# The first two weight units after two of the norms are multiplied together, chunk by chunk, into four PSUM banks

## What is computed

```python
# first block: gated short convolution, then a squared-relu MLP
a = modulate(rmsnorm(h, g_pre), shift, scale)
h = h + gate * rmsnorm(short_gated_conv(a, w_in, conv, w_out), g_post)
f = squared_relu_mlp(modulate(rmsnorm(h, g_pre_ff), s2, c2), mlp_w_in, mlp_w_out)   # 1024 -> 4096 -> 1024
h = h + gate2 * rmsnorm(f, g_post_ff)
# second block, layer 0: forgetting attention and pooling, then a convolutional feed-forward
z = rms_norm(h, even_norm) @ even_w_in          # q, k, v, forget logit, pool input
h = h + concat(attention(q, k, v, cumsum(log_sigmoid(f + b))), pool(u)) @ even_w_out
h = h + conv_ffn(rms_norm(h, ffn_norm0))
# layer 1: conformer convolution, then a feed-forward
```

## Time and profile before

| what | value |
|---|---|
| runs, median (lowest to highest) | 1940.53 us (1940.49 to 1945.62), 3 runs |
| profiled execution, span | 1940.5 us |
| time around the span in that execution | none that the profile shows |
| PE busy | 1759.1 us, 91% |
| DVE busy | 1133.7 us, 58% |
| ACT busy | 705.6 us, 36% |
| chain that ended last | PE 86%, DVE 6%, ACT 3% |

### The profile page before, as it was taken

The page is one execution under the profiler, slowest core; times in us unless marked ns, Lnnn a source line. Parts: engine busy times, 40 slices in busy tenths (PEclk is TensorE's granted clock), DMA queues, the critical chain, the costliest instruction groups (busy, mean ns, idle before and its releaser), DMA issues.

```text
span 1940.5 us, 22187 instructions
## 1 busy us (share of the span) xinstructions
PE 1759.1 (91%) x7628; PEld 1411.7 (73%) x7628; DVE 1133.7 (58%) x1740; ACT 705.6 (36%) x1003; POOL 21.1 (1%) x52
## 2 busy tenths in 40 slices
PE   5899949999999499679899999989996989999997
PEld 4788838888888278567688888867652768888886
DVE  5698655343344653444664573757997567466364
ACT  2222235232222434542552442434323455234232
POOL 0000000000000000300000000000000000000000
PEclk7799879999999699899899999999997989999999
DMA  6576302332324022001223223232210222323221
GB/s 227 172 225 227 112 22 87 91 104 87 108 87 125 22 87 88 22 0 52 68 97 109 87 86 108 76 97 66 65 43 22 65 65 86 108 87 107 89 92 60
DMA packets 172276, 176.01 MB, mean 91 GB/s; under 512 B 2984, under 2 KB 171180, under 8 KB 172220
## 3 DMA queue, kind: packets, MB, share of 16 engines
q1 hardware_dynamic: 172220, 175.29, 28.2%
HBM read 173.15 MB, written 2.10 MB: 90 GB/s over the span
## 4 chain that ended last, share of the span: by engine, by line
PE 86%; DVE 6%; ACT 3%; issue 2%; DMA 1%; DVEq 0%; SPq 0%; ACTq 0%
PE PSUM L1128 25%; PE PSUM L1129 25%; PE PSUM L1130 25%; PE PSUM L1301 3%; DVE SQ L698 1%; PE PSUM L1254 1%; PE PSUM L1156 1%; PE PSUM L1148 1%; PE PSUM L1271 1%; DMA XROW<-in_x 1%; DVE X L747 1%; PE PSUM L1195 1%; DMA ARAW<-in_ada_w 1%; ACT L413 1%; PE PSUM L1255 0%
## 5 line engine op out<-in xcount | busy, mean ns | idle before, releaser
L1128 PE MATMUL PSUM<-XH,WH 128*128 128x512 f32 x1504 | 594.1, 395 | 30.9 <-DVE XL L729 15.2
L1129 PE MATMUL PSUM<-XL,WH 128*128 128x512 f32 x1504 | 589.4, 392 | 0.0
L1130 PE MATMUL PSUM<-XH,WL 128*128 128x512 f32 x1504 | 589.2, 392 | 0.0
L390 ACT ACTIVATE WH<-RAW 128x1024 fp32r<-128x1024 f32 x280 | 287.3, 1052 | 826.9 <-PE PSUM L1130 810.8
L1128 PEld LDWEIGHTS PSUM<-XH,WH 128*128 128x128 f32 x1504 | 285.4, 190 | 98.5 <-issue 39.4
L685 DVE TENSOR_TENSOR WL<-RAW,WH 128x1024 fp32r<-128x1024 f32 x280 | 335.4, 1222 | 17.7 <-ACT WH L390 17.7
L1129 PEld LDWEIGHTS PSUM<-XL,WH 128*128 128x128 f32 x1504 | 285.4, 190 | 61.0 <-issue 1.9
L1130 PEld LDWEIGHTS PSUM<-XH,WL 128*128 128x128 f32 x1504 | 284.9, 189 | 59.9
L1128 PE MATMUL PSUM<-HH,WH 128*128 128x512 f32 x672 | 264.6, 394 | 6.2 <-DVE HL L1007 5.8
L1129 PE MATMUL PSUM<-HL,WH 128*128 128x512 f32 x672 | 264.0, 393 | 0.0
L1130 PE MATMUL PSUM<-HH,WL 128*128 128x512 f32 x672 | 263.6, 392 | 0.0
(11 more groups left out here) (181 smaller groups left out, 1389.6 us busy)
## 6 DMA issues: line engine op xcount, KB each, us to landing
RAW<-in_ffn_w_up SPq DMA_DIRECT2D x44, 1024.0 KB, 5.1
ARAW<-in_ada_w SPq DMA_DIRECT2D x24, 1024.0 KB, 5.2
RAW<-in_mlp_w_in SPq DMA_DIRECT2D x16, 1024.0 KB, 5.7
RAW<-in_mlp_w_out SPq DMA_DIRECT2D x16, 1024.0 KB, 5.2
RAW<-in_ffn_w_down SPq DMA_DIRECT2D x16, 1024.0 KB, 5.1
RAW<-in_sc_w_in SPq DMA_DIRECT2D x12, 1024.0 KB, 5.2
RAW<-in_odd_w_pw SPq DMA_DIRECT2D x12, 1024.0 KB, 5.3
RAW<-in_even_w_in SPq DMA_DIRECT2D x8, 1024.0 KB, 5.8
```

What stands on the lines that cost most here:

```text
L390: act.activation(WH[:, j, a:b, :], RAW[:, j, a:b, :], ACT.Copy).then_inc(s_hi, 1)
L1128: pe.matmul(o, wh, mh[:, k, :], start=(k == 0), stop=False)
L1129: pe.matmul(o, wh, ml[:, k, :], start=False, stop=False)
L1130: mm = pe.matmul(o, wl, mh[:, k, :], start=False, stop=(k == kn - 1))
```

## The change

The preparation of the second unit of each of the two stages (units 17 and 49) moves ahead of the split: on ACT before `split_shift` and `split`, on DVE behind the first two scalings and ahead of the first `XL`. On PE a new function `two_units` takes units 16 and 17 (48 and 49) together: it waits until all banks are empty and both units' weights are complete, goes through chunks 0 to 4 with both units (12 matmuls per chunk, four banks), then through chunks 5 to 7 with the first unit, counts up `s_mm`, and through 5 to 7 with the second. The units 18, 19, 50 and 51 follow with `product` one by one, written out where they were in a hardware loop.

```diff
--- before.py
+++ after.py
@@ -465,8 +465,8 @@
             for c in range(DC):
                 square(ST_X1, c, X[:, c, :])
             rms(ST_X1, 1.0 / D)
+            prep_late(U_MLP + 1)
             split_shift(1, S_GS1, S_MOD + 24)
-            prep_late(U_MLP + 1)
 
 
             for g in range(4):
@@ -501,8 +501,8 @@
             rms(ST_X2, 1.0 / D)
             act.wait_ge(s_fw, 16)
             act.activation(FH[:, :, :], FRAW[:, :, :], ACT.Copy).then_inc(s_fh, 1)
+            prep_late(U_EVEN + 1)
             split(2, "even_norm", 0)
-            prep_late(U_EVEN + 1)
 
 
             act.wait_ge(e_f, 1)
@@ -712,7 +712,7 @@
                     dve.wait_ge(s_as, 7 * (summed(a)[0] - 1) + k)
                     stt(dst, w, s, dst, ALU.mult, ALU.add).then_inc(s_as if k < 7 else s_ad, 1)
 
-            def split(m, gs=None, gain=None, k=0):
+            def split(m, gs=None, gain=None, k=0, late=None):
 
                 dve.wait_ge(s_r, (ST_X0, ST_X1, ST_X2, ST_F0, ST_X3, ST_F1)[m] + 1)
 
@@ -721,6 +721,8 @@
 
                 scaled(0)
                 scaled(1)
+                if late is not None:
+                    prep_late(late)
                 for c in range(DC):
                     dve.wait_ge(sp_h, 8 * m + c + 1)
                     if gain is None:
@@ -854,8 +856,7 @@
                     tt(sc_(S_MG1, 8), sc_(S_MOD + 40, 8), col("gains", 24, 8), ALU.mult).then_inc(s_sm, 1)
                     dve.wait_ge(s_sm, 7)
             post_norm(ST_Y0, 0, S_MG0)
-            split(1)
-            prep_late(U_MLP + 1)
+            split(1, late=U_MLP + 1)
 
 
             for g in range(4):
@@ -884,8 +885,7 @@
             post_norm(ST_Y1, 1, S_MG1)
             dve.wait_ge(s_fh, 1)
             tt(FL[:, :, :], FRAW[:, :, :], FH[:, :, :].bitcast(F32), ALU.subtract).then_inc(s_fl, 1)
-            split(2, gain="even_norm")
-            prep_late(U_EVEN + 1)
+            split(2, gain="even_norm", late=U_EVEN + 1)
 
 
             dve.wait_ge(s_vin2, 16)
@@ -1130,6 +1130,24 @@
                         mm = pe.matmul(o, wl, mh[:, k, :], start=False, stop=(k == kn - 1))
                 mm.then_inc(s_mm, 1)
 
+            def two_units(u, base_):
+
+                pe.wait_ge(s_ev, u)
+                for j in range(2):
+                    pe.wait_ge(s_lo, (u + j) * 2 + 2)
+                for first, last, units in ((0, 5, (0, 1)), (5, 8, (0,)), (5, 8, (1,))):
+                    for k in range(first, last):
+                        pe.wait_ge(s_x, base_ + k + 1)
+                        for j in units:
+                            for c in range(2):
+                                wh, wl = (w[:, j, k, c * P:c * P + P] for w in (WH, WL))
+                                o = PS_[:, 2 * j + c, :]
+                                pe.matmul(o, wh, XH[:, k, :], start=(k == 0), stop=False)
+                                pe.matmul(o, wh, XL[:, k, :], start=False, stop=False)
+                                mm = pe.matmul(o, wl, XH[:, k, :], start=False, stop=(k == 7))
+                    if last == 8:
+                        mm.then_inc(s_mm, 1)
+
             def x_units(u0, n, base_):
 
                 with pe.Fori(0, n // 2) as it:
@@ -1199,7 +1217,12 @@
             channel_sum(ST_Y0)
             channel_sum(ST_X1)
             for g in range(4):
-                x_units(U_MLP + 8 * g, 4, 8)
+                if g == 0:
+                    two_units(U_MLP, 8)
+                    for j in range(2):
+                        product(U_MLP + 2 + j, j, XH, XL, 8, s_x, 8)
+                else:
+                    x_units(U_MLP + 8 * g, 4, 8)
                 h_units(U_MLP + 8 * g + 4, 4, 8 + 8 * g)
             channel_sum(ST_Y1)
             channel_sum(ST_X2)
@@ -1213,7 +1236,9 @@
                 pe.matmul(o, FH[:, k, :], XL[:, k, :], start=False, stop=False)
                 mm = pe.matmul(o, FL[:, k, :], XH[:, k, :], start=False, stop=(k == 7))
             mm.then_inc(s_f, 1)
-            x_units(U_EVEN, 4, 16)
+            two_units(U_EVEN, 16)
+            for j in range(2):
+                product(U_EVEN + 2 + j, j, XH, XL, 8, s_x, 16)
             def head_sums(n0):
 
                 for n in (n0, n0 + 1):
```

## The result

The changed kernel takes 1945.66 us (median of 20 runs, 1944.02 to 1947.27). The kernel before, run beside it, takes 1943.01 us (20 runs, 1939.43 to 1945.62). The ratio is 1.0014, 95% interval 1.0008 to 1.0021: 2.7 us slower, between 1.6 and 4.1 us. It is within the 0.3% that was called no change, and it is slower, as forecast.

A forecast was written before the change was run, and what follows sets the result against it. PE, at 91% of the span, was taken as the bound, with its waits ahead of first matmuls. Delays of 1.5 and 2.2 us less 0.2 us of clock gave +3.5 us on 1940.5 us: 1944.0 us, range 1942.0 to 1946.0 us.

The forecast's parts named there:

- The reordering is worth nothing: Reordering the 96 matmuls of the two units on PE gains and costs 0, in both stages.
- +1.5 us in stage 1: Before the MLP: preparation moved ahead of the split delays the first XL by 1.5 us.
- +2.2 us in stage 2: Before the even layer's projections: DVE's moved subtractions delay the first XL by 2.2 us.
- rival 1: Units 18 and 50: weights' lower halves come late, both stages lose 1.3 us, 1946.6 us in all; chance 6%.
- rival 2: Both stages' 96 matmuls drop to 1.2 GHz while four banks are cycled: 34 us more, 1978 us; chance 1%.
- The clock's term, -0.2 us: Slow PE stretches at four stages' first matmuls, redrawn by the shift: 13.85 us instead of 14.2 us, -0.2 us.
- the forecast's ends: Clock extremes for the four slow stretches: all at 2.69 us, -1.6 us; all at 4.83 us, +2.4 us.
- The absolute time: Whole kernel: 1944.0 us, from +3.5 us on 1940.5 us, with span and median time taken as alike.
- rival 4: Both stages: joint order fills PE's waits between chunks, 1.5 us in all, delay stays, 1942.5 us; chance 3%.

The follow-up runs named there:

- e3: Kernel before with the preparation of units 17 and 49 moved into ACT's and DVE's gaps further ahead, PE's old order; 1942.89 us, ratio 1.0000.
- e2: Changed kernel (two units together) with the preparation of units 17 and 49 moved still further ahead, into ACT's and DVE's gaps; 1943.63 us, ratio 0.9998.
- e4: Like e2, two units together, plus the split of stage 2's forget weight done early; 1940.55 us, ratio 0.9993 to the kernel before.
- e5: Like e3, old order, plus the split of stage 2's forget weight done early; 1941.29 us, ratio 0.9990 to the kernel before.
- e7: Same slowed stage 1 chunks as e6, but the two units multiplied together as in the changed kernel; 1942.64 us, ratio 0.9995.
- e9: e4 (two units together) plus unused matmuls keeping PE busy ahead of the split in both stages; 1938.04 us, ratio 0.9971.
- e8: e5 (old order) plus unused matmuls keeping PE busy ahead of the split in both stages; 1938.14 us, ratio 0.9973.
- e1: Changed kernel's earlier preparation of units 17 and 49 only, PE multiplying units one after the other as before; 1944.43 us, ratio 1.0009.
- e6: Preparation in the gaps, old order, with two unused DVE scalings added per chunk in stage 1 to slow the chunks; 1947.26 us, ratio 1.0022.
- e10: e8 plus 18 unused matmuls ahead of each of the three later splits (two feed-forwards, convolution), old order; 1932.21 us, ratio 0.9951.

## Why the prediction was right, point by point

- *The reordering is worth nothing.* Right, and shown. From the first matmul of stage 1 to the window of unit 18 (L867 at 327.55 before) it is 35.36 us before, 34.43 us after, 34.98 us in e3 with the old order and the preparation in the gaps. Less 0.47 of the slow stretch of each (4.83, 2.70 and 3.97 us) these are 33.1, 33.2 and 33.1 us. e2 against e3 and e4 against e5 differ by 0.7 us in either direction, within their intervals. e7 shows the condition that was missing.
- *+1.5 us in stage 1 and +2.2 us in stage 2.* Right in mechanism, 0.25 and 0.2 us too large: 1.25 and 2.00 us. The durations of neighbours on DVE overlap by 0.08 or 0.09 us in the trace (in stage 1 the subtractions start at 289.92, where 288.71 + 1.29 is 290.00), once ahead of the inserted pair and once behind it, and the working added full durations: 2.36 - 0.94 - 0.17 = 1.25 and 2.36 - 0.19 - 0.17 = 2.00. e2 and e3 show that the delay goes when the work is moved.
- *The third unit's weights (rival 1).* Didn't happen: 2.7 us needed, as predicted, 4.1 us of cover.
- *The clock falls with four banks (rival 2).* Didn't happen. After 296.15 the 0.23 us between matmuls hold, with four banks in turn, and PE has no idle time between them; in the changed kernel the window from 300 to 310 has granted 1.00, as before.
- *The clock's term, -0.2 us.* Its place was incomplete and its sign, at the first matmuls, came out the other way. It looked at first matmuls, four of them, and there the rule taken from the Trainium skill ("TensorE: Matmul & The Clock Gate", What's actually happening), that the switch isn't tied to the kernel's work, fits: 4.83 us became 2.70 us when the first matmul came 0.83 us later, and before the first feed-forward the stretch stayed at 2.69 us (938.35 to 941.04). Before the convolution 2.70 us became 5.26 us, longer than any stretch the forecast's ends had allowed for, and before the second feed-forward it stayed near 3.97 us (1564.93 to 1568.91). The four make 14.6 us in place of 14.2 us: +0.2 us, not -0.2 us. The channel sums (0.95 us each), the attention (1.2 us) and the convolution's taps (1.3 us) draw too and were left out. In the profiled pair the sum of all draws is 2.0 - 3.25 = -1.25 us. Over 20 runs against 20 the ratio gives 2.7 us, so -0.6 us remain, less than the interval is wide. That the forecast's -0.2 us is not far from it is luck: the draws are of about 1 us each and of either sign, and most of them stand where the term didn't look.
- *The absolute time.* 1944.0 us stood on a median of three runs, 1940.53 us; over 20 runs the kernel before has 1943.0 us. Of the 1.7 us between forecast and result, 2.5 us are this shift of the median and -0.8 us the change's own smaller size (2.7 us for 3.5 us). The prediction took span and time to be alike because both read 1940.5; they are not. In every execution on record the time is 1.7 to 2.5 us longer than the core's span (the changed kernel's profiled one: 1944.65 us, span 1942.5 us), so the profiled execution of before was one of about 1942.5 us. The result stands 0.3 us inside the range's upper end. On the base of 20 runs the same sum gives 1946.5 us, 0.8 us above the result; that the low base and the too large delay partly cancel is luck.
- *Faster by over 0.3% as the form promises (rival 4).* Didn't happen; its bound for the fast clock, 0.3 us in stage 1, is what e9 against e8 shows.

What stays open: what decides a draw. That the draws make the spread is on record, since each run has its mean granted clock. Of 33 runs of the kernel before beside e1, e2, e3 and e5, the nine with 0.944 took 1939.6 to 1940.7 us and the eleven with 0.941 took 1944.5 to 1945.8 us. An estimate from these rows agrees: 0.003 less of 1940 us, at half speed, is 11.6 us more at the lower level, which costs 0.47 of that, 5.5 us. But the clock by place is known for the profiled executions alone. And the times don't tell e1 from the changed kernel (1.2 us between medians, each beside other runs of before); only their traces do.

## What to carry to other kernels

Before two products are interleaved to fill an engine's waits, look where these waits stand: a wait ahead of the first instruction is latency, which more work per chunk can't fill, and work that is moved up to make the interleaving possible lengthens it. Such preparation belongs where its engine waits for something else, here between the squares and ahead of R. And where a serial stretch leaves PE at its lower clock, unused matmuls paced by waits brought 0.17% in two stages and 0.39% in five (ratios of e8 and e10 over that of e5), where the joint order brought nothing.

## What the runs showed that was not expected

- A channel sum's two matmuls take 1.12 or 2.07 us after the same idle time of 2.98 us, at the same place of two executions; each draw is 0.95 us on the serial path. The slow stretch before the convolution was 2.70 us in one and 5.26 us in the other, 1.2 us of difference.
- DVE operations shown with 0.69 us follow each other every 0.60 us when none waits (e6), so a sum over their durations is 15% too large here.
- In e10, before the first feed-forward, PE's channel sum was itself partly slow (1.78 us, from 923.00), then came the 18 unused matmuls in 6.12 us, and the first chunk found the upper level (0.23 us between matmuls from 930.17 on).
- The mean granted clock of a run goes with its time: 0.944 with 1939.6 to 1940.7 us and 0.941 with 1944.5 to 1945.8 us in the kernel before.
